# Recurrent states and outputs of a gated linear attention stage: another order on TensorE, state sums on another engine

## The chip, the cores and the metric

The kernel runs on one core of one Trainium2 chip. The metric is the device time of one execution in microseconds (us). TensorE (PE) multiplies matrices; its weight loads are shown as an engine of their own (PEld). VectorE (DVE), ScalarE (ACT) and GpSimd (POOL) work on whole tiles of 128 partitions; SyncE (SP) and ScalarE issue transfers. Matrix products land in PSUM. Everything here is float32.

## The reference

It is one step of a two-layer encoder over 656 tokens: a prompt of 528 (16 learned ones and 512 frames, from an empty state) and eight continued sequences of 16 tokens, each with a state of its own. Layer 0 mixes by gated linear attention (GLA), layer 1 by a gated short convolution; a causal convolutional feed-forward net of width 2816 follows each. The change touches only the GLA mixer, and of it what comes after the score matrices. For each of 4 heads (keys of 128, values of 256) the reference computes, for a block of tokens with start state S,

```python
def gla_chunk(S, q, k, v, g):
    b = jnp.cumsum(g, axis=1)
    o_inter = einsum('bthd,bhde->bthe', q * exp(b), S)
    ...
    A = einsum('bthd,bshd,btshd->bhts', q, k, decay)
    o_intra = einsum('bhts,bshe->bthe', A, v)
    b_last = b[:, -1]
    k_dec = k * exp(b_last[:, None] - b)
    S_new = exp(b_last)[..., None] * S + einsum('bshd,bshe->bhde', k_dec, v)
    return S_new, o_inter + o_intra
...
o = o * rsqrt(mean(o * o, axis=-1) + EPS) * head_gain      # the head norm
o = o.reshape(B, L, GLA_HV) * silu(r)
return o @ w_out, S
```

The states after the prompt (one a head) and after each sequence (eight a head) are outputs of the kernel too.

## The kernel before, in words

**Layout.** Activations lie as [128 channels, tokens]; 656 tokens are one tile row. A projection (`project`, L420) multiplies one unit of weights, 8 tiles of 128x128, with a high and a low part of both operands (three products each), 48 matmuls. Nearly the whole kernel is such units (196 of them), streamed in a ring of four.

**PSUM.** It is cut into four slots of two banks (1024 floats a partition). `plan_slots` hands them out in the order in which TensorE uses them, round robin: each step takes the next slot. Before a step TensorE waits in `open_slot` until the engine that read the slot's former content has raised `freed`. So the order of the steps also decides whose reader a step waits for: it is always the fourth step before it.

**The stage of states and outputs** comes after the last projection of values and gates (r, head 3, half 1) and its last score matrices A. The prompt is cut into four chunks of 128 tokens and a tail of 16. For each head h, TensorE does, in the order of `plan_slots`:

- U0: four updates, keys (tokens on partitions, tile `kd`) times values (`v_tok`), one of each chunk, [128 tokens] x [128 keys, 256 values] (L574)
- U1: four updates for sequences 0 to 3. The sample's 128 tokens are one tile; `kd` holds four copies of it, in each of which all but every fourth sequence is multiplied by zero (`C_FOURTH`), so that a matmul over 64 partitions gives the update of a single sequence
- the tail's update over 16 partitions, then U2 with sequences 4 to 7
- the head norm's sum of the head before (`head_norm(h-1)`, L582): ones times `osum`
- the transposes of the next head's keys (kT, L536)
- o0 and o1, the two halves of the outputs (L622): per chunk A times values and query times state (`chain`), and for each of the eight sequences a matmul of 16 columns with its old state (`s0`)

Slots, written as step: step whose reader frees it. In heads 1 and 2, head norm: U0, kT: U1, o0: tail, o1: U2, next U0: head norm.

**VectorE**, per head: `chain` (L975, L978: the running prompt state, one copy and three multiply-adds out of U0), four new states out of U1 (L991: old state times decay plus update), the tail's state (L998), four out of U2, then `finish(h-1)` (the inverse root of the head norm by one Newton step, L788 to L798, and two multiplications into `qk`, L967), then both halves of the outputs times gain and gate (`o32`, L1007) and the sum of squares `osum` (L1011).

**ScalarE**, per head: `head_root(h-1)` (logarithm and exponential, each time after a load of its table set), `k_to_tokens(h+1)` (kT out of PSUM into `kd`: one copy and four scaled copies, L1320, L1322), the stores of the states, the squares of both output halves (L1380), and `split_out(h-1)` (`oh`, L1241). At the head's end it issues the load of the states of head h+2. **GpSimd** subtracts `ol` = `qk` - `oh` (L378), which with `oh` is the input of w_out. The first projections of w_out (L646) take the k-th of 8 tiles when `o_done` says that `ol` is there.

**Ahead of the stage**, in head 3: ScalarE applies silu to the two gates with a table set of its own between the exponentials of the decays (`gate_r`), VectorE multiplies decays into k and q (`decayed`, steps 7 and 8) after the last gate, and the old states of heads 0 and 1 are loaded (L1358) into the space of the layer's input `xh` once the last projection is over.

Of the kernel before, what the change touches and what calls it, by code (L numbers as in the profile page):

```python
# [28 lines left out]
P = 128  # L29
# [21 lines left out]
RING = 4  # L51
# [25 lines left out]
C_FOURTH = 76  # L77
# [41 lines left out]
def plan_slots():  # L119
# [10 lines left out]
    for h in range(HEADS):  # L130
        s.straight(("U", h, 0), ("U", h, 1), ("U", h, "tail"), ("U", h, 2))
        if h:
            s.straight(("head_norm", h - 1))
        if h + 1 < HEADS:
            s.straight(("kT", h + 1))
        s.straight(("o", h, 0), ("o", h, 1))
# [27 lines left out]
def build(nc, x_in, w_in, wgd_in, wgu_in, par_in, reset_in, mask_in, s0_in, zc_in,  # L164
# [6 lines left out]
    def sb(name, shape, dt=F32, offset=None, size=None):  # L171
# [4 lines left out]
        for d in shape[1:]:  # L176
# [55 lines left out]
    kd = sb("kd", [P, 9, P], offset=b_at)  # L232
    chain = sb("chain", [P, 5, DV], offset=b_at + 9 * 4 * P)
    assert 9 * 4 * P + 5 * 4 * DV <= HEADS * T4
# [28 lines left out]
             "lev_done", "r_silu", "dec_done", "chain_stored", "osq_done", "osum_done", "o_done", "o_scaled", "oh_done", "x_back",  # L263
# [89 lines left out]
    def _(pool):  # L353
# [22 lines left out]
        for k in range(KT):  # L376
            pool.wait_ge(sem["oh_done"], k + 1)
            pool.tensor_tensor(ol[:, k, :], qk[:, k, :], oh[:, k, :].bitcast(F32),  # L378
                               ALU.subtract).then_inc(sem["o_done"], 1)
# [14 lines left out]
    def _(pe):  # L394
# [16 lines left out]
        def project(step, hi, lo, n_ready, ring, first=0, cut=HALF, i=0, release=1, before=None):  # L411
# [3 lines left out]
            for k in range(KT):  # L415
                if before:
                    before(k)
                for w, v in ((wh, hi), (wh, lo), (wl, hi)):
                    for c, a, z in banks(first, cut):
# [3 lines left out]
                        if k == 0 and w is wh and v is hi and c and release:  # L423
                            mm.then_inc(sem["units_used"], release)
            mm.then_inc(filled[p], 1)
# [113 lines left out]
        def value(kind, h, e):  # L539
            nonlocal n_unit  # L540
            project((kind, h, e), xh, xl, n_unit + 1, n_unit % RING)
            n_unit += 1
# [42 lines left out]
        for h in range(HEADS):  # L585
# [10 lines left out]
            for j in (1, 2):  # L596
                if j == 2:
                    open_slot(("U", h, "tail"))
                    mm, p = update(h, "tail", 0, kd[0:16, 4, :], v_tok[0:16, 4, vs])
                    mm.then_inc(filled[p], 1)  # L600
                open_slot(("U", h, j))
                for n in range(4):
                    s = 4 * (j - 1) + n
                    rows = slice(64 * (s // 4), 64 * (s // 4) + 64)
                    mm, p = update(h, j, n, kd[rows, 5 + s % 4, :], v_tok[rows, 5, vs])
                mm.then_inc(filled[p], 1)
            if h:
                head_norm(h - 1)
            if h + 1 < HEADS:
                transpose_k(h + 1)  # L610
            copied(("U", h, 0))
# [147 lines left out]
    def _(dve):  # L759
# [178 lines left out]
        for h in range(HEADS):  # L938
# [7 lines left out]
            for n, (kind, e) in enumerate((("v", 0), ("v", 1), ("r", 0), ("r", 1))):  # L946
                take_value(kind, h, e)
# [4 lines left out]
                decayed(h, 2 * n + 1)  # L952
# [6 lines left out]
                decayed(h, 2 * n + 2)  # L959
# [9 lines left out]

        dve.wait_ge(sem["dec_done"], HEADS)  # L970
        for h in range(HEADS):
            if h:
                dve.wait_ge(sem["chain_stored"], 16 * h)
# [10 lines left out]
            dve.wait_ge(s0_in_s[h % 2], 16 * (h // 2 + 1))  # L984
            if h >= 2:
                dve.wait_ge(snew_stored[h % 2], 16)
            for s in range(SEQS):
                n = s % 4
                if n == 0:
                    p = take(("U", h, 1 + s // 4))  # L990
                ins = dve.scalar_tensor_tensor(out=snew[:, h % 2, s, :], in0=s0[:, h % 2, s, :],  # L991
                                               scalar=dec[:, h, 5 + s:6 + s], in1=ps[:, p, n * DV:(n + 1) * DV],
                                               op0=ALU.mult, op1=ALU.add)
                if n == 3:
                    ins.then_inc(freed[p], 1)
                if s == 3:
                    p = take(("U", h, "tail"))
                    dve.scalar_tensor_tensor(out=chain[:, 4, :], in0=chain[:, 3, :], scalar=dec[:, h, 4:5],  # L998
                                             in1=ps[:, p, 0:DV], op0=ALU.mult, op1=ALU.add).then_inc(freed[p], 1)
            if h:  # L1000
                finish(h - 1)
            for e in range(2):
                p = take(("o", h, e))
                dve.wait_ge(sem["osq_done"], 2 * h + e + 1)
                if e == 0:
# [4 lines left out]
                                         op1=ALU.mult).then_inc(freed[p], 1)  # L1010
            dve.tensor_tensor(osum[:, :], osq[:, 0, :], osq[:, 1, :], ALU.add).then_inc(sem["osum_done"], 1)  # L1011
        finish(HEADS - 1)
        dve.wait_ge(sem["x_back"], 16)
# [188 lines left out]
    def _(act):  # L1202
# [23 lines left out]
        def root(step, r, d):  # L1226

            act.preload_act_table_set(LOG_EXP)
            inverse_root(two(r), slot(take(step)), r, d)
# [4 lines left out]
        def head_root(h):  # L1234
            root(("head_norm", h), head_std, DV)
# [82 lines left out]
        def k_to_tokens(h):  # L1318
            p = take(("kT", h))
            act.copy(kd[:, 0:5, :], blocks(ps[:, p, 0:5 * P], P))  # L1320
            for j in range(4):
                last = act.activation(kd[:, 5 + j, :], ps[:, p, 5 * P:6 * P], ACT.Copy,  # L1322
                                      scale=par[:, C_FOURTH + j:C_FOURTH + j + 1])
# [6 lines left out]
        for h in range(HEADS):  # L1330
# [13 lines left out]
            gate_r(h, 0)  # L1344
# [3 lines left out]
            gate_r(h, 1)  # L1348
            if h + 1 < HEADS:
                high(u + 3)  # L1350
# [8 lines left out]

        take(("r", HEADS - 1, 1))  # L1360
        load_states(0)
        load_states(1)
# [285 lines left out]
```

## Time and profile before

| | us |
|---|---|
| median of 3 timed runs | 1551.24 |
| lowest and highest | 1548.32, 1552.26 |
| the profiled execution's own time | 1546.99 |
| its span, first to last instruction | 1545.2 |
| TensorE busy in it | 1523.1 (99%) |
| VectorE, ScalarE, GpSimd busy | 1028.9, 441.1, 562.3 |

The profiled execution took 1.8 us more than its span. All times of rows are from the start of that span. A matmul of float32 operands is recorded as two instructions, each with a weight load: "x26" are 13 products. Ends of matmuls are modelled, and TensorE is shown busy where a matmul waits in the array, so the starts of the weight loads (PEld) tell the pace better. "[0.33 <-issue]" is idle time before an instruction for which no releaser was found. PEclk is the share of TensorE's full clock that was granted.

### The profile page before, as it was taken

The numbers are of one execution on the slowest core, as the hardware profiler recorded it, in microseconds if no ns is written. First come the engines' busy times: TensorE is split into PE (matmuls) and PEld (weight loads), VectorE is DVE, ScalarE is ACT, GpSimd is POOL, SyncE is SP. The second block draws the span as 40 slices with busy tenths as digits, with TensorE's granted clock in tenths as the row PEclk, the third lists the DMA queues.
The fourth block names the chain that finished last, engine by engine and source line by source line (L and its number), as shares of the span: only waits on it lengthen the run. The fifth ranks groups of instructions, "written<-read, shape, count | busy, mean of one in ns | idle before, by whom it ended". The sixth has DMA issues, their size and how long they took to land.

```text
span 1545.2 us, 26347 instructions
## 1 busy us (share of the span) xinstructions
PE 1523.1 (99%) x10294; PEld 1505.0 (97%) x10294; DVE 1028.9 (67%) x1495; ACT 441.1 (29%) x692; POOL 562.3 (36%) x397
## 2 busy tenths in 40 slices
PE   7999999999999999999999999999999999999997
PEld 6999998899999999999999999999999999999996
DVE  6566665744976676666669535548976676667667
ACT  5355554343222212212125111115221212212213
POOL 3532221143343434334342343432443344334340
PEclk9999999999999999999999999999999999999998
DMA  6211116222222222222221322222222222222212
GB/s 220 78 55 56 55 55 240 89 66 77 69 69 82 68 81 65 70 81 68 81 70 55 107 82 69 71 80 73 71 79 75 76 81 66 70 81 68 82 42 79
DMA packets 34841, 123.76 MB, mean 80 GB/s; under 512 B 3888, under 2 KB 6832, under 8 KB 33616
## 3 DMA queue, kind: packets, MB, share of 16 engines
q1 hardware_dynamic: 31840, 108.37, 22.0%
q10 hardware_dynamic: 2928, 14.35, 2.5%
q8 instruction: 54, 0.88, 0.2%
q14 instruction: 19, 0.16, 0.0%
HBM read 114.48 MB, written 8.22 MB: 79 GB/s over the span
## 4 chain that ended last, share of the span: by engine, by line
PE 96%; DVE 2%; ACT 1%; DVEq 1%; DMA 0%; POOL 0%; issue 0%; SPq 0%; ACTq 0%
PE ps L420 64%; PE ps L436 22%; PE ps L522 2%; PE ps L622 2%; PE ps L721 1%; PE ps L574 1%; PE ps L646 1%; PE ps L536 1%; DMA raw<-w_units 0%; DVE x L1177 0%; PE ps L656 0%; PE ps L503 0%; ACT xh L1214 0%; PE ps L493 0%; DVE sq L781 0%; DVEq L976 0%
## 5 line engine op out<-in xcount | busy, mean ns | idle before, releaser
L365 POOL TENSOR_TENSOR wl<-raw,wh 128x512 fp32r<-128x512 f32 x380 | 546.0, 1461 | 883.6 <-ACT wh L1260 846.9
L420 PE MATMUL ps<-xh,wh 128*128 128x320 f32 (+2 forms) x2144 | 494.5, 312 | 0.0
L420 PE MATMUL ps<-xl,wh 128*128 128x320 f32 (+2 forms) x2144 | 491.3, 310 | 0.0
L420 PE MATMUL ps<-xh,wl 128*128 128x320 f32 (+2 forms) x2144 | 490.8, 310 | 0.0
L420 PEld LDWEIGHTS ps<-xl,wh 128*128 128x128 f32 x2144 | 372.1, 188 | 0.0
L420 PEld LDWEIGHTS ps<-xh,wh 128*128 128x128 f32 x2144 | 369.9, 188 | 0.7
L420 PEld LDWEIGHTS ps<-xh,wl 128*128 128x128 f32 x2144 | 370.3, 188 | 0.0
L1260 ACT ACTIVATE wh<-raw 128x1024 fp32r<-128x1024 f32 x196 | 204.3, 1055 | 317.9 <-PE ps L420 294.4
L812 DVE TENSOR_TENSOR x<-ps,x 128x320 f32<-128x320 f32 (+2 forms) x320 | 167.5, 569 | 107.0 <-PE ps L436 78.1
L1025 DVE SCALAR_TENSOR_TENSOR y<-zp,par,y 128x660 f32<-128x660 f32 (+1 forms) x192 | 181.5, 945 | 28.0 <-issue 23.2
L436 PE MATMUL ps<-gh,wh 128*128 128x320 f32 (+1 forms) x768 | 175.6, 310 | 0.0
L436 PE MATMUL ps<-gh,wl 128*128 128x320 f32 (+1 forms) x768 | 175.1, 309 | 0.0
L436 PE MATMUL ps<-gl,wh 128*128 128x320 f32 (+1 forms) x768 | 174.8, 309 | 0.0
L1405 ACT COPY zl<-zp 128x18 f32 (+1 forms) x88 | 18.3, 208 | 533.5 <-DVE y L1025 533.5
L436 PEld LDWEIGHTS ps<-gh,wh 128*128 128x128 f32 x768 | 129.2, 188 | 0.0
L436 PEld LDWEIGHTS ps<-gl,wh 128*128 128x128 f32 x768 | 129.2, 188 | 0.0
L436 PEld LDWEIGHTS ps<-gh,wl 128*128 128x128 f32 x768 | 128.4, 188 | 0.0
L1021 DVE TENSOR_SCALAR y<-zp,par 128x660 f32<-128x660 f32 (+1 forms) x96 | 71.8, 748 | 29.8 <-issue 26.9
L1038 DVE TENSOR_TENSOR gl<-hh,gh 128x644 fp32r<-128x644 f32 (+1 forms) x52 | 84.0, 1615 | 3.9
L1044 DVE TENSOR_TENSOR zp<-ps,rstd 128x520 f32<-128x520 f32 x44 | 30.6, 696 | 58.6 <-PE ps L420 58.5
L1047 DVE TENSOR_TENSOR zp<-ps,rstd 128x320 f32<-128x320 f32 x44 | 21.5, 488 | 56.0 <-PE ps L420 55.8
L1036 DVE CAST gh<-hh 128x644 fp32r<-128x644 f32 (+1 forms) x52 | 48.2, 927 | 3.8
(160 smaller groups left out, 1283.6 us busy)
## 6 DMA issues: line engine op xcount, KB each, us to landing
raw<-w_units SPq DMA_DIRECT2D x196, 512.0 KB, 3.5
s<-states ACTq DMA_DIRECT2D x4, 1024.0 KB, 5.1
state_sample<-snew ACTq DMA_DIRECT2D x4, 1024.0 KB, 4.2
x<-x_t SPq DMA_DIRECT2D x8, 328.0 KB, 8.3
x<-x_t ACTq DMA_DIRECT2D x1, 2624.0 KB, 10.6
y_t<-x SPq DMA_DIRECT2D x4, 384.0 KB, 2.4
y_t<-x SPq DMA_DIRECT2D x4, 256.0 KB, 2.2
ffn_last<-zl ACTq DMA_DIRECT2D x2, 396.0 KB, 3.4
```

The source lines that it names most:

```text
L365: last = pool.tensor_tensor(wl[:, j, ks, :], raw[:, j, ks, :], wh[:, j, ks, :].bitcast(F32), ALU.subtract)
L420: mm = pe.matmul(ps[:, p, c:c + z - a], w[:, ring, k, :], v[:, k, a:z], start=(k == 0 and w is wh and v is hi), stop=(k == KT - 1 and w is ...
L436: mm = pe.matmul(ps[:, p, c:c + z - a], w[:, rings[f], m, :], v[:, f0 + f, a:z], start=(f == 0 and w is wh and v is gh), stop=(f == 1 and ...
L522: return pe.matmul(queries(ps[:, p, :], a, z), ks[:, a:a + P], queries(qs, a, z), start=True, stop=True)
L622: return pe.matmul(ps[:, p, a:z], lhsT, rhs, start=start, stop=stop, skip_group_check=True)
L812: last = dve.tensor_tensor(tile, product, tile, ALU.add)
L1021: dve.tensor_scalar(out, src[:, first:YN], w_col(0), w_col(3) if bias else None, ALU.mult, ALU.add if bias else ALU.bypass)
L1025: last = dve.scalar_tensor_tensor(out=out, in0=src[:, first + j:YN + j], scalar=w_col(j), in1=out, op0=ALU.mult, op1=ALU.add)
L1036: dve.tensor_copy(gh[:, f, first:TOK], hh[:, first:TOK])
L1038: dve.tensor_tensor(gl[:, f, first:TOK], hh[:, first:TOK], gh[:, f, first:TOK].bitcast(F32), ALU.subtract).then_inc(sem["g_done"], 1)
L1044: dve.tensor_tensor(two(zp[:, zi, 2 + first:SB]), slot(p, cut - first), two(factor[:, first:PROMPT]), ALU.mult)
L1260: act.activation(wh[:, j, :, :], raw[:, j, :, :], ACT.Copy).then_inc(sem["hi_done"], 1)
```

## The change

- **Order on TensorE and slots**: per head now U0, tail, head norm of the head before, key transposes, then U1 and U2, then o0 and o1. By the rule of the fourth step before, in heads 1 and 2 U1 now takes the slot of U0, U2 that of the tail, o0 that of the head norm, o1 that of kT; the next U0 takes that of U1, the next tail that of U2.
- **Sequence updates**: `kd` holds two masked copies in place of four (even and odd sequences, `C_PARITY`). Each update spans 32 partitions, two sequences of which one is zero. The eight go out in the order of partitions 0, 32, 64, 96 for the even sequences, then again for the odd ones; the four of a round write to four PSUM banks. Both slots are opened before the first of them.
- **New states**: ScalarE multiplies the old states by their decay into `snew` (`scale_states`, eight activations of 128x256 per head), and VectorE adds U1 and U2 in two additions of 128x1024. The tail's state is computed ahead of these, and has a buffer for even and for odd heads, so that `chain` waits only for the store of two heads ago.
- **ol**: the subtractions move from GpSimd to VectorE (`low_out`), between the two output halves of the next head; ScalarE's `split_out` moves to between its two squares.
- **Tables and loads**: only the first head norm loads its table set. In head 3 both silus come after the exponentials, `decayed` 7 and 8 before the last gate is taken, and the loads of the old states are issued when the last projection has used the first tiles of its input (semaphore `inputs_used`, raised after tiles 3 and 6).
- `k_to_tokens(h+1)` now also waits for U2 of head h, as `kd` is read longer.

```diff
     for h in range(HEADS):
-        s.straight(("U", h, 0), ("U", h, 1), ("U", h, "tail"), ("U", h, 2))
+        s.straight(("U", h, 0), ("U", h, "tail"))
...
             s.straight(("kT", h + 1))
-        s.straight(("o", h, 0), ("o", h, 1))
+        s.straight(("U", h, 1), ("U", h, 2), ("o", h, 0), ("o", h, 1))
...
     osum = sb("osum", [P, TOK], offset=xh_at + 32768 + 2 * T4)
-    kd = sb("kd", [P, 9, P], offset=b_at)
-    chain = sb("chain", [P, 5, DV], offset=b_at + 9 * 4 * P)
-    assert 9 * 4 * P + 5 * 4 * DV <= HEADS * T4
+    kd = sb("kd", [P, 7, P], offset=b_at)
+    chain = sb("chain", [P, 6, DV], offset=b_at + 7 * 4 * P)
+    assert 7 * 4 * P + 6 * 4 * DV <= HEADS * T4
...
                 low(j, RING * i + (RING + j + 1))
-        for k in range(KT):
-            pool.wait_ge(sem["oh_done"], k + 1)
-            pool.tensor_tensor(ol[:, k, :], qk[:, k, :], oh[:, k, :].bitcast(F32),
-                               ALU.subtract).then_inc(sem["o_done"], 1)
...
             assert done % RING == u % RING == 0
...
-        def project(step, hi, lo, n_ready, ring, first=0, cut=HALF, i=0, release=1, before=None):
+        def project(step, hi, lo, n_ready, ring, first=0, cut=HALF, i=0, release=1, before=None, marks=()):
...
             weights(n_ready)
...
                             mm.then_inc(sem["units_used"], release)
+                if k in marks:
+                    mm.then_inc(sem["inputs_used"], 1)
...
         def project_down(step, first, f0, n_ready, rings, i=0, release=1, g_count=None):
...
             nonlocal n_unit
-            project((kind, h, e), xh, xl, n_unit + 1, n_unit % RING)
+            project((kind, h, e), xh, xl, n_unit + 1, n_unit % RING,
+                    marks=(3, 6) if (kind, h, e) == ("r", HEADS - 1, 1) else ())
...
         def transpose_v(h, e):
...
             mm.then_inc(filled[p], 1)
-            for j in (1, 2):
-                if j == 2:
-                    open_slot(("U", h, "tail"))
-                    mm, p = update(h, "tail", 0, kd[0:16, 4, :], v_tok[0:16, 4, vs])
-                    mm.then_inc(filled[p], 1)
-                open_slot(("U", h, j))
-                for n in range(4):
-                    s = 4 * (j - 1) + n
-                    rows = slice(64 * (s // 4), 64 * (s // 4) + 64)
-                    mm, p = update(h, j, n, kd[rows, 5 + s % 4, :], v_tok[rows, 5, vs])
-                mm.then_inc(filled[p], 1)
+            open_slot(("U", h, "tail"))
+            mm, p = update(h, "tail", 0, kd[0:16, 4, :], v_tok[0:16, 4, vs])
+            mm.then_inc(filled[p], 1)
...
                 transpose_k(h + 1)
+            open_slot(("U", h, 1))
+            open_slot(("U", h, 2))
+            for odd in range(2):
+                for group in range(4):
+                    rows = slice(32 * group, 32 * group + 32)
+                    mm, p = update(h, 1 + group // 2, group % 2 * 2 + odd, kd[rows, 5 + odd, :], v_tok[rows, 5, vs])
+                    if odd and group % 2:
+                        mm.then_inc(filled[p], 1)
...
             pe.wait_ge(sem["lev_done"], 9 * h + 9)
...
             for n, (kind, e) in enumerate((("v", 0), ("v", 1), ("r", 0), ("r", 1))):
+                early = n == 3 and h == HEADS - 1
+                if early:
+                    dve.drain()
+                    decayed(h, 7)
+                    decayed(h, 8)
...
                     distance(h, 2 * n + 2)
-                decayed(h, 2 * n + 1)
+                if not early:
+                    decayed(h, 2 * n + 1)
...
                     distance(h, 2 * n + 3)
-                decayed(h, 2 * n + 2)
+                if not early:
+                    decayed(h, 2 * n + 2)
...
+        def low_out(h):
+
+            for k in (2 * h, 2 * h + 1):
+                dve.wait_ge(sem["oh_done"], k + 1)
+                dve.tensor_tensor(ol[:, k, :], qk[:, k, :], oh[:, k, :].bitcast(F32),
+                                  ALU.subtract).then_inc(sem["o_done"], 1)
...
         for h in range(HEADS):
-            if h:
-                dve.wait_ge(sem["chain_stored"], 16 * h)
+            if h > 1:
+                dve.wait_ge(sem["chain_stored"], 16 * (h - 1))
...
             dve.drain()
...
                 dve.drain()
-            dve.wait_ge(s0_in_s[h % 2], 16 * (h // 2 + 1))
-            if h >= 2:
-                dve.wait_ge(snew_stored[h % 2], 16)
-            for s in range(SEQS):
-                n = s % 4
-                if n == 0:
-                    p = take(("U", h, 1 + s // 4))
-                ins = dve.scalar_tensor_tensor(out=snew[:, h % 2, s, :], in0=s0[:, h % 2, s, :],
-                                               scalar=dec[:, h, 5 + s:6 + s], in1=ps[:, p, n * DV:(n + 1) * DV],
-                                               op0=ALU.mult, op1=ALU.add)
-                if n == 3:
-                    ins.then_inc(freed[p], 1)
-                if s == 3:
-                    p = take(("U", h, "tail"))
-                    dve.scalar_tensor_tensor(out=chain[:, 4, :], in0=chain[:, 3, :], scalar=dec[:, h, 4:5],
-                                             in1=ps[:, p, 0:DV], op0=ALU.mult, op1=ALU.add).then_inc(freed[p], 1)
+            p = take(("U", h, "tail"))
+            dve.scalar_tensor_tensor(out=chain[:, 4 + h % 2, :], in0=chain[:, 3, :], scalar=dec[:, h, 4:5],
+                                     in1=ps[:, p, 0:DV], op0=ALU.mult, op1=ALU.add).then_inc(freed[p], 1)
+            dve.wait_ge(sem["states_scaled"], h + 1)
+            for j in range(2):
+                p = take(("U", h, 1 + j))
+                states = snew[:, h % 2, 4 * j:4 * j + 4, :].rearrange("p s v -> p (s v)")
+                dve.tensor_tensor(states, ps[:, p, :], states, ALU.add).then_inc(freed[p], 1)
...
             for e in range(2):
...
                                          op1=ALU.mult).then_inc(freed[p], 1)
+                if h and e == 0:
+                    low_out(h - 1)
...
         finish(HEADS - 1)
+        low_out(HEADS - 1)
...
         update_x(lambda m: ("w_out", m), FIRST_ATT, 1)
...
-        def root(step, r, d):
-
-            act.preload_act_table_set(LOG_EXP)
+        def root(step, r, d, load=True):
+
+            if load:
+                act.preload_act_table_set(LOG_EXP)
...
         def head_root(h):
-            root(("head_norm", h), head_std, DV)
+            root(("head_norm", h), head_std, DV, load=h == 0)
...
             p = take(("kT", h))
+            if h:
+                take(("U", h - 1, 2))
             act.copy(kd[:, 0:5, :], blocks(ps[:, p, 0:5 * P], P))
-            for j in range(4):
+            for j in range(2):
                 last = act.activation(kd[:, 5 + j, :], ps[:, p, 5 * P:6 * P], ACT.Copy,
-                                      scale=par[:, C_FOURTH + j:C_FOURTH + j + 1])
+                                      scale=par[:, C_PARITY + j:C_PARITY + j + 1])
...
         def gate_r(h, e):
...
                 k_to_tokens(0)
-            gate_r(h, 0)
+            else:
+                gate_r(h, 0)
...
             decay(h, 7)
-            gate_r(h, 1)
             if h + 1 < HEADS:
+                gate_r(h, 1)
...
             act.activation(dec[:, h, 0:4], blocks(b[:, h, 0:TAIL], CH)[:, :, CH - 1], ACT.Exp, scale=1.0 / TAU)
...
+        def scale_states(h):
+
+            act.wait_ge(s0_in_s[h % 2], 16 * (h // 2 + 1))
+            if h >= 2:
+                act.wait_ge(snew_stored[h % 2], 16)
+            for n in range(SEQS):
+                last = act.activation(snew[:, h % 2, n, :], s0[:, h % 2, n, :], ACT.Copy,
+                                      scale=dec[:, h, 5 + n:6 + n])
+            last.then_inc(sem["states_scaled"], 1)
+
+        for h in range(2):
+            act.wait_ge(sem["inputs_used"], h + 1)
+            load_states(h)
+        gate_r(HEADS - 1, 0)
+        gate_r(HEADS - 1, 1)
+        act.drain()
         take(("r", HEADS - 1, 1))
-        load_states(0)
-        load_states(1)
+        scale_states(0)
...
         act.drain()
...
             copied(("U", h, 2))
-            act.dma_start(sp_out[:, h, :], chain[:, 4, :]).then_inc(sem["chain_stored"], 16)
+            act.dma_start(sp_out[:, h, :], chain[:, 4 + h % 2, :]).then_inc(sem["chain_stored"], 16)
             act.dma_start(ss_out[:, h, :, :], snew[:, h % 2, :, :]).then_inc(snew_stored[h % 2], 16)
+            if 0 < h < HEADS - 1:
+                scale_states(h + 1)
...
                 act.activation(osq[:, e, :], ps[:, p, 0:TOK], ACT.Square).then_inc(sem["osq_done"], 1)
-            if h:
-                split_out(h - 1)
+                if e == 0 and h:
+                    split_out(h - 1)
+                if e == 0 and h == 0:
+                    scale_states(1)
...
         act.dma_start(zc[:, :, :], zc_in).then_inc(sem["zc_in"], 16)
...
     par[:, C_CCACHE:N_PAR] = a["cache_conv"][0].reshape(SEQS, 2, KT, P).transpose(3, 2, 0, 1).reshape(P, -1)
-    for j in range(4):
-        par[:, C_FOURTH + j] = np.arange(P) // SLEN % 4 == j
+    for j in range(2):
+        par[:, C_PARITY + j] = np.arange(P) // SLEN % 2 == j
...
     wgu = np.concatenate([a["gla_w_gate_up"][0]] * 2)
```

## Rows read from the trace of the kernel before

**Rows 1.** The page: header, and shares by engine of the last chain.

```profile
span 1545.2 us, 26347 instructions
PE 96%; DVE 2%; ACT 1%; DVEq 1%; DMA 0%; POOL 0%; issue 0%; SPq 0%; ACTq 0%
```

**Rows 2.** Windows by head: start:end, length, busy each engine, PEclk, DMA share, GB/s.

```profile
239.30:255.30 16.00, 15.88 (x107) 13.55 (x106) 8.32 (x17) 5.92 (x12) 2.51 (x2) 1.00 0.97 369
255.30:275.20 19.90, 19.90 (x109) 16.57 (x109) 13.14 (x22) 5.90 (x10) 0.00 (x0) 0.83 0.38 142
275.20:292.30 17.10, 16.95 (x110) 14.16 (x109) 14.11 (x22) 7.18 (x12) 3.71 (x2) 1.00 0.35 131
292.30:308.80 16.50, 16.36 (x104) 13.57 (x103) 14.11 (x22) 5.55 (x7) 3.70 (x2) 1.00 0.18 72
```

**Rows 3.** Timeline, head 2, TensorE: start, us, engine, line, operation, operands, count.

```profile
275.23 6.44 PE L574 MATMUL ps<-v_tok,kd 128*128 128x256 f32 x26
...
277.13 1.59 PEld L574 LDWEIGHTS ps<-v_tok,kd 64*128 64x128 f32 x8 [0.33 <-issue]
...
279.68 1.59 PEld L574 LDWEIGHTS ps<-v_tok,kd 64*128 64x128 f32 x8 [0.33 <-issue]
...
281.60 1.37 PE L582 MATMUL ps<-osum,ones 128*128 128x328 f32 x4
...
283.12 0.85 PE L536 MATMUL ps<-ident,qk 128*128 128x128 f32 x6
...
283.80 0.61 PE L622 MATMUL ps<-AT,v_tok 128*128 128x128 f32 x4
```

**Rows 4.** Timeline, head 2, the other engines.

```profile
275.42 0.72 ACT L1380 ACTIVATE osq<-ps 128x656 f32<-128x656 f32 x1 [5.15 <-PE ps L622]
...
276.24 0.90 DVE L1007 SCALAR_TENSOR_TENSOR o<-ps,par,sr 128x656 f32<-128x656 f32 x1 [4.31 <-ACT osq L1380]
...
276.85 3.71 POOL L378 TENSOR_TENSOR ol<-qk,oh 128x656 fp32r<-128x656 f32 x2 [30.29 <-ACT oh L1241]
277.05 2.07 DVE L1011 TENSOR_TENSOR osum<-osq 128x656 f32<-128x656 f32 x1
...
279.05 0.41 DVE L975 COPY chain<-ps 128x256 f32<-128x256 f32 x1
...
279.53 1.59 DVE L978 SCALAR_TENSOR_TENSOR chain<-chain,dec,ps 128x256 f32<-128x256 f32 x3
...
281.32 1.66 DVE L991 SCALAR_TENSOR_TENSOR snew<-s,dec,ps 128x256 f32<-128x256 f32 x4 [0.19 <-issue]
...
282.89 0.47 DVE L998 SCALAR_TENSOR_TENSOR chain<-chain,dec,ps 128x256 f32<-128x256 f32 x1
...
284.85 0.90 DVE L788 TENSOR_SCALAR osum<-ps,par 128x656 f32<-128x656 f32 x1
```

**Rows 5.** Timeline, head 1: the same sum of squares with GpSimd idle.

```profile
257.08 0.83 DVE L1011 TENSOR_TENSOR osum<-osq 128x656 f32<-128x656 f32 x1
```

**Rows 6.** Groups by form, all four heads: count, busy us, mean ns, idle before.

```profile
L574 PE MATMUL ps<-v_tok,kd 64*128 64x256 f32 x64 | 16.4, 397 | 0.0
```

**Rows 7.** Timeline, head 0: sixteen weight loads for products of 16 columns.

```profile
249.13 1.87 PEld L622 LDWEIGHTS ps<-qk,s 128*128 128x128 f32 x16
```

**Rows 8.** Timeline, head 0: end of U0; ScalarE's scaled copies.

```profile
241.18 1.59 PEld L574 LDWEIGHTS ps<-v_tok,kd 64*128 64x128 f32 x8 [0.33 <-issue]
...
247.15 1.15 ACT L1322 ACTIVATE kd<-ps,par 128x128 f32<-128x128 f32 x4
```

**Rows 9.** DMA issues around the stage: KB each, median us to landing.

```profile
s<-states ACTq DMA_DIRECT2D x4, 1024.0 KB, 5.1
```

**Rows 10.** Window of 4 us in which the granted clock fell.

```profile
254.00:258.00 4.00, 4.00 (x21) 3.26 (x20) 1.65 (x2) 2.00 (x2) 0.00 (x0) 0.74 1.04 376
```

**Rows 11.** Timeline, w_out after head 3: GpSimd's ol and TensorE's wait for it.

```profile
310.46 3.75 POOL L378 TENSOR_TENSOR ol<-qk,oh 128x656 fp32r<-128x656 f32 x2 [12.80 <-ACT oh L1241]
...
314.27 0.30 PEld L646 LDWEIGHTS ps<-oh,wh 128*128 128x128 f32 x2 [1.00 <-POOL ol L378]
```

More of the change, by code:

```diff
@@ L76 @@
 C_SCW = 52
-C_FOURTH = 76
+C_PARITY = 76
 C_EPS, C_HALF_EPS = 80, 81
@@ L262, in build @@
              "xs_hi", "xs_lo", "sq_done", "sum_done", "log_done", "root_done", "soft_done", "mask_in", "d_done", "e_done",
-             "lev_done", "r_silu", "dec_done", "chain_stored", "osq_done", "osum_done", "o_done", "o_scaled", "oh_done", "x_back",
+             "lev_done", "r_silu", "dec_done", "inputs_used", "states_scaled", "chain_stored", "osq_done", "osum_done", "o_done", "o_scaled", "oh_done", "x_back",
              "zc_in", "pads_in", "y_done", "zl_saved", "gate_silu", "g_done", "cpads_in", "cy_done",
```

## The prediction, made before the changed kernel was run

> **What bounds the kernel now.** I read the page first. TensorE carries 96% of the chain that ended last in a span of 1545.2 us [rows 1], so only what shortens or lengthens TensorE's own sequence counts. The change touches the stretch from the first state update to the first w_out units. The windows by head divide it: 16.0, 19.9, 17.1 and 16.5 us for heads 0 to 3 [rows 2]. They show TensorE busy all through, but its records hide waits inside the array, so I read the timeline of one undisturbed head, head 2, by the starts of the weight loads. With T = 275.23, where its updates start: U0 is over at T+1.9, U1, tail and U2 at T+6.4, the head norm's sum runs 1.4 us, kT starts at T+7.9, the outputs at T+8.5 [rows 3], and the next head at T+17.1, so the outputs take 8.6. TensorE's own work thus sets the pace; kT alone waited a moment, for VectorE's states. VectorE in the same head: square of o1 until 276.14, o32 until 277.14, osum until 279.12, chain from 279.05 to 281.12, four states from 281.32 to 282.98, tail at 282.89, half_square (L788) at 284.85 [rows 4].
>
> **Step 1: the slots, and what TensorE waits for now.** All of head h in heads 1 and 2, T as above.
> VectorE: o32 ends at T+1.9 as before. osum took 2.07 beside GpSimd's ol [rows 4] and 0.83 with GpSimd idle [rows 5]; ol leaves GpSimd, so I take 0.83: osum ends at T+2.65. The chain's 2.07 us run from T+2.6 to T+4.7, then 0.2 for the drain (281.12 to 281.32) and 0.47 for the tail: T+5.35.
> TensorE: U0 1.9, tail 0.63 (U2's load at 279.68, less U1's at 277.13 and U1's 1.92), so T+2.55. The head norm waits for osum until T+2.8 and takes 1.37, kT 0.66: T+4.8. U1 and U2 now need the slots of U0 and the tail, both opened first: they wait until T+5.35+0.14 = T+5.5 (0.14 lies between the states' end at 282.98 and kT at 283.12).
> The eight updates: see step 2, 1.9 or 3.4 us; the last ends at T+7.4 or T+8.9.
> Then the new wait: o0 takes the slot of the head norm, which VectorE frees with half_square, and half_square stands behind both additions. An addition of 128x1024 is not in the trace; from 0.47 us at 256 columns and 0.90 at 656 [rows 4] it is 0.47 + 768 x 0.00107 = 1.3 us, two back to back 2.45. Bounds: 1.9, if they cost no more per column than the 0.83 of osum at 656, with start-up shared, and 2.6. The first starts when U1 is filled, at six of the eight updates: T+7.0 or T+8.1. Additions to T+9.4 or T+10.5, half_square to T+10.2 or T+11.4, outputs from T+10.3 or T+11.5, next head at T+18.9 or T+20.1. Before it was 17.1. So heads 1 and 2 lose 1.8 each, 3.6 together, or 3.0 each, 6.0 together. Queued behind the waiting o0 is all of TensorE; the stall of some 2.7 us stands in nobody's cover. The head norm's logarithm on ScalarE can start at T+4.2, needs about the 0.72 of a square, and is not late.
>
> **Step 2: do updates of different partitions overlap?** The trace has none in such an order. Lower end of their speed: instructions over 64 partitions have 397 ns each [rows 6], and U1's eight take 1.9 us as U0's over 128 do [rows 3]: a product on fewer rows is no cheaper, 0.213 us per instruction, eight products 3.4 us. Upper end: where products are short (16 columns), sixteen weight loads follow in 1.87 us [rows 7], 0.11 each; the sixteen loads of eight updates can't come faster, 1.8 us. Each float32 product is two instructions on the same rows, which must follow each other, while the next product's first has other rows and another bank free: a pipeline two wide, 8 x 0.213 + 0.2 = 1.9 us. I take 1.9, at the end of the row of weight loads, since the order leaves nothing shared between neighbours but that load path; 3.4 is the rival's.
> The Trainium skill (TensorE: Matmul & The Clock Gate, Part 3) says that products at different row groups run concurrently, 3.07 times as fast for four of 32 rows and 512 columns; by that figure, estimated, the eight would take 1.1 us instead of 3.4 and the sum below would be 3 us lower. No row of this case shows it. On the other side TensorEngine Tiling (Key Properties) says that changing the tiling mode drains the array; the trace agrees: each change between 128 and fewer partitions shows 0.33 us before the load [rows 3], and there are four a head before and after, which changes nothing.
>
> **Step 3: heads 0 and 3.** Head 0: U0 is over at 241.2 [rows 8]; q and k are ready earlier than before, so the chain runs 241.2 to 243.3, the updates from 243.4 to 245.3 (or 246.8), the outputs 8.7: 254.0 (or 255.5) against 255.3. Gain 1.3 (or loss 0.2). The additions need scale_states: eight activations of 256 columns, 0.39 each (0.29 at 128, 1.15 for four [rows 8], 0.72 at 656), 3.1 us on ScalarE after the states land. Their load is issued before 239 and takes 5.1 [rows 9], so they are scaled at 245 to 247, and kT's copy after them is done before o1 wants its slot at 249.7. If they land later, o1 waits 1 or 2 us. In later heads this lies beside the outputs and costs nothing. Head 3 has no kT: o0 has the tail's slot, o1 the head norm's, so it waits for the chain alone: updates from T+4.8 to T+6.7 (8.3), outputs to T+15.5 (17.0) against 16.5. Gain 1.0 (loss 0.5).
>
> **Step 4: the clock.** From 254 to 258, after output products of 16 columns, the mean grant was 0.74 [rows 10]; over head 1 it was 0.83, which is 6.8 us at the level of 1.2 GHz, and head 1 took 19.9 where head 2 at 2.4 GHz took 17.1 [rows 2]: 2.8 us. Afterwards heads 1 and 2 have some 0.7 and 2.8 us without work ahead of their outputs, so I expect half as much again, 10 us at the lower level, +1.4. Bounds: none of it, -2.8, and two and a half times as much, +4.2.
>
> **Step 5: the end.** TensorE waited 1.0 us for ol behind 3.75 us of GpSimd [rows 11]. On VectorE ol of head 2 is done before the last head's outputs end: -1.0. ol of head 3 takes VectorE 0.83 each (as osum) in place of GpSimd's 1.9, so it is earlier, beside the same early products of w_out that hid it before. ScalarE's dropped table loads and copies and the earlier loads lie beside TensorE and are worth nothing but step 3's.
>
> **Sum**, overlapping: +3.6 - 1.3 - 1.0 + 1.4 - 1.0 = +1.7 us. The profiled execution's own time, 1546.99, lies 4.3 under the median of the runs, which is above all of the difference; I add to the median: 1551.24 + 1.7 = 1553.
>
> **The rivals.**
> A, the forecast, updates overlap two wide: +1.7, 1553 (its own range 1549 to 1556), chance 0.46.
> B, the slower side: the updates do not overlap. +6.0 + 0.5 + 0.2 + 0.7 (the idle time before the outputs is a little shorter) - 1.0 = +6.4, 1557.6. It decides from the point where the eight updates take over 3 us. For it: 397 ns at 64 partitions. Against: those never alternated. 0.27.
> C, faster: four updates overlap fully (1.0 us, -0.9 in each of 4 heads) and the clock never falls (-4.2 against step 4): 1.7 - 3.6 - 4.2 = -6.1, 1545. For it: heads 2 and 3 ran whole at full clock. Against: idle time is added, and a float32 product's two halves use the same rows. 0.17. The rule of the Trainium skill in step 2 (TensorE: Matmul & The Clock Gate, Part 3) is on its side.
> D: the updates overlap as in A, but the stalls bring the lower clock in every head, and the state load is late: +4.2 - 1.4 + 1.5 on A's 1.7, +6.0, 1557. 0.10.
>
> **The numbers.** About 0.3% (4.7 us) is what a measurement of this kernel can tell from no change. Faster: C and a little of A, 0.20. Slower: B and D less what falls inside, and A's edge, 0.33. Same 0.47. Range 1545 to 1560: it holds A, B, D and the near half of C.
>
> **What would show it.** Right, if in heads 1 and 2 o0's first weight load follows the last update by over 2 us and starts with the end of L788; if the sixteen update instructions of U1 and U2 start within 2 us; if osum takes 0.83 everywhere; and if no wait stands in the first w_out unit. Heads 1 and 2 near 19 us, 0 near 15, 3 near 15.5. Wrong, if the outputs start before half_square ends, or if additions of 1024 columns take well under 1.2 us.

## The result, and the profile after

The changed kernel is slower: 1557.64 us median (1555.28 to 1563.45, 19 runs) against 1548.32 us (1542.67 to 1553.60, 19 runs), ratio 1.0068 with a 95% interval of 1.0055 to 1.0081, some 10.5 us; the two medians lie 9.3 us apart. The forecast was 1553 in a range of 1545 to 1560, "the same" at 0.47 and slower at 0.33. Ratios are to the kernel before, timed beside each kernel, and the difference between two changed kernels is that of their ratios. Two disturbed executions, one of the kernel before at 6330.47 us and one of a variant at 1574.75, are left out of the ratios. The page of the profiled execution, its header and the shares of the last chain:

```profile
span 1557.5 us, 26352 instructions
PE 96%; DVE 2%; ACT 1%; DVEq 1%; DMA 0%; issue 0%; SPq 0%; ACTq 0%
```

The span grew by 12.3 us, and TensorE is still the chain [rows 1]. The windows of heads 0 to 3 and of the first three w_out units say where (columns as in [rows 2]):

```profile
238.70:254.30 15.60, 14.66 (x106) 12.91 (x106) 6.05 (x9) 9.96 (x22) 2.49 (x2) 0.89 0.80 289
254.30:278.40 24.10, 19.91 (x111) 17.56 (x111) 13.59 (x18) 10.07 (x18) 0.00 (x0) 0.72 0.37 150
278.40:306.90 28.50, 25.08 (x109) 21.28 (x109) 13.68 (x18) 8.82 (x18) 0.00 (x0) 0.57 0.21 79
306.90:322.40 15.50, 15.09 (x103) 12.47 (x104) 12.17 (x17) 4.46 (x6) 0.00 (x0) 0.90 0.19 77
322.40:345.00 22.60, 22.60 (x150) 22.25 (x150) 12.17 (x16) 6.22 (x9) 0.00 (x0) 1.00 0.09 33
```

Heads 1 and 2 took 52.6 us in place of 37.0 [rows 2]; heads 0 and 3 gained 1.4 together, the first units of w_out 1.2 (22.6 against 23.8), and the stage starts 0.6 earlier. The granted clock is the column that changed most: 0.72 and 0.57. A grant of 0.50 is 1.2 GHz and one of 1.00 is 2.4 GHz, so in each window (1 - grant) x length x 2 is the time at the lower level: 3.4, 13.5, 24.5 and 3.1, together 44 us where it was 6.8.

The timeline of head 1 (T = 254.27), TensorE and VectorE, to be read against [rows 3, 4]:

```profile
254.27 1.60 PEld L573 LDWEIGHTS ps<-v_tok,kd 128*128 128x128 f32 x8
...
256.12 0.83 DVE L1018 TENSOR_TENSOR osum<-osq 128x656 f32<-128x656 f32 x1
...
257.07 0.85 PEld L581 LDWEIGHTS ps<-osum,ones 128*128 128x128 f32 x4 [0.58 <-issue]
...
259.05 0.48 DVE L998 SCALAR_TENSOR_TENSOR chain<-chain,dec,ps 128x256 f32<-128x256 f32 x1
...
259.65 0.77 PEld L573 LDWEIGHTS ps<-v_tok,kd 32*128 32x128 f32 x16 [0.79 <-DVE chain L991]
259.68 1.15 PE L573 MATMUL ps<-v_tok,kd 32*128 32x256 f32 x16 [0.58 <-DVE chain L998]
...
260.92 2.36 DVE L1004 TENSOR_TENSOR snew<-ps,snew 128x1024 f32<-128x1024 f32 x2 [1.39 <-PE ps L573]
...
263.19 0.89 DVE L787 TENSOR_SCALAR osum<-ps,par 128x656 f32<-128x656 f32 x1
...
264.23 1.20 PE L621 MATMUL ps<-AT,v_tok 128*128 128x128 f32 x4 [3.40 <-DVE osum L787]
```

The reader is to see two things. The last row names its releaser: the outputs waited 3.40 us for half_square (L787), which stood behind the two additions (L1004). And the eight updates, sixteen instructions, took 1.15 us. What came after the wait stands in the chain that ended last (start, us, what), both output halves of heads 1, 2 and 3:

```profile
264.23 14.15 PE ps L621 x72
...
290.50 16.33 PE ps L621 x72
...
313.72 8.72 PE ps L621 x72
```

The same 72 instructions take 8.7 us at full clock, and 1.6 and 1.9 times as long behind the two waits.

Finer windows show where the clock fell and came back (start:end and length as above, the granted clock third from the end):

```profile
246.70:250.70 4.00, 4.00 (x29) 4.00 (x28) 0.90 (x1) 2.25 (x6) 1.60 (x2) 0.72 1.04 415
...
270.70:274.70 4.00, 4.00 (x20) 4.00 (x20) 1.31 (x2) 1.99 (x3) 0.00 (x0) 0.50 0.00 0
274.70:278.70 4.00, 4.00 (x29) 3.72 (x29) 1.09 (x2) 0.28 (x1) 0.00 (x0) 0.87 0.00 0
278.70:282.70 4.00, 4.00 (x10) 2.39 (x10) 3.02 (x5) 0.43 (x1) 0.00 (x0) 0.56 0.73 262
...
302.70:306.70 4.00, 4.00 (x21) 4.00 (x20) 0.00 (x0) 0.00 (x0) 0.00 (x0) 0.50 0.00 0
```

There are four spells at the lower level. Two of them began inside the two waits and lasted some 13.6 and 20.5 us, 34 of the 44; in the second of these TensorE was busy without a break from 290.5 to 309.9 and the clock stayed down. The other two began while TensorE was busy: 3.4 us in the outputs of head 0, and 6.8 us from U0 of head 2, after the clock had come back before the outputs of head 1 were over. Spells of that shorter kind stand in the kernel before as well, as [rows 10] shows one.

### The profile page after: what moved, and what is told of

It is laid out like the page before. It is cut to its first block, busy times and chain, and to the rows that moved or that the text cites. A ratio compares the mean times of both kernels' runs of the same rounds, so it can differ in the third digit from the quotient of the medians.

```text
span 1557.5 us, 26352 instructions
## 1 busy us (share of the span) xinstructions
PE 1528.1 (98%) x10294; PEld 1511.4 (97%) x10294; DVE 1028.4 (66%) x1479; ACT 444.7 (29%) x710; POOL 547.9 (35%) x389
## 4 chain that ended last, share of the span: by engine, by line
PE 96%; DVE 2%; ACT 1%; DVEq 1%; DMA 0%; issue 0%; SPq 0%; ACTq 0%
PE ps L416 63%; PE ps L434 22%; PE ps L621 3%; PE ps L520 2%; PE ps L720 1%; PE ps L645 1%; PE ps L573 1%; PE ps L534 0%; DMA raw<-w_units 0%; DVE x L1185 0%; PE ps L655 0%; PE ps L501 0%; ACT xh L1222 0%; PE ps L491 0%; DVEq L792 0%; DVE sq L780 0%
```

## The experiments

Of each kernel "lower-clock time" is worked out from its windows as above. Theory W and rival C are those of the expectations below; this rival C is not the prediction's.

**half_square ahead of the additions.** Base: the changed kernel.

```diff
             p = take(("U", h, "tail"))
 ...
+            if h:
+                q = take(("head_norm", h - 1))
+                half_square(..., two(osum[:, :]), slot(q), DV).then_inc(freed[q], 1)
             dve.wait_ge(sem["states_scaled"], h + 1)
             for j in range(2):
...
-            inverse_root(("head_norm", h), head_std, osum[:, :], DV)
+            refine(ROOT_ORDER.index(("head_norm", h)), head_std, osum[:, :])    # heads 0 to 2
```

> Only VectorE's order changes: half_square of the head norm before goes ahead of the two additions of 128x1024, so the slot that o0 wants in heads 1 and 2 is freed by about T+6.3 instead of T+9.9. Theory W (the wait for half_square starts the loss, the lower clock follows from the idle time): o0 starts some 0.2 us after the last update, 3.4 us of wait go in each of two heads, most of the lower clock with them (under 12 us at the lower level in the stage, against 44 in the changed kernel); heads 1 and 2 near 15.5 us each; time 14 to 18 us below the changed kernel, 5 to 9 below the one before. Rival C (the clock falls because the updates are now only 1.15 us of dense work and the outputs with 16 columns are not enough, whatever waits there are): the wait goes, -7 us, but the outputs stay at the lower clock, heads 1 and 2 at 19 to 22 us; time 7 us below the changed kernel, 2 to 3 above the one before.

Measured: 1540.80 us against 1547.02 for the kernel before, ratio 0.9953 (0.9935 to 0.9970), 6 runs. That is 1.15% or 18 us below the changed kernel and 7 us below the one before; it beats both. Windows of its heads 0 to 3:

```profile
238.90:253.00 14.10, 13.16 (x106) 11.51 (x106) 6.05 (x9) 9.91 (x22) 2.49 (x2) 1.00 0.81 292
253.00:268.10 15.10, 14.32 (x110) 12.23 (x110) 12.44 (x17) 9.96 (x18) 0.00 (x0) 1.00 0.66 265
268.10:285.60 17.50, 17.50 (x110) 14.05 (x110) 13.69 (x19) 8.69 (x17) 0.00 (x0) 0.80 0.34 129
285.60:301.10 15.50, 15.23 (x103) 12.48 (x104) 13.82 (x19) 4.50 (x6) 0.00 (x0) 0.89 0.19 77
```

and in its head 1 the outputs now follow the updates at once, with the additions beside them:

```profile
258.24 1.15 PE L573 MATMUL ps<-v_tok,kd 32*128 32x256 f32 x16 [0.58 <-DVE chain L1001]
259.31 0.52 PEld L621 LDWEIGHTS ps<-AT,v_tok 128*128 128x128 f32 x4 [0.33 <-issue]
...
259.48 2.36 DVE L1010 TENSOR_TENSOR snew<-ps,snew 128x1024 f32<-128x1024 f32 x2 [0.57 <-PE ps L573]
```

Lower-clock time is 10 us, as expected under 12. Theory W holds, rival C (outputs stay slow) falls: the outputs of heads 1 to 3 took 8.7 us each. But head 2 took 17.5 us and not 15.5, since the spells that are left begin at the end of a head's outputs, about the U0 of heads 2 and 3, with TensorE busy.

**Keep TensorE busy in the wait.** Base: the changed kernel. It computes seven products that nobody reads.

```diff
+            if h in (1, 2):
+                pk, _ = slots.at(("kT", h + 1))
+                for _ in range(7):
+                    mm = pe.matmul(ps[:, pk, 768:1024], ones[:, :], v_tok[:, 0, vs], start=True, stop=True, ...)
+                mm.then_inc(filled[pk], 1)        # kT of heads 2 and 3 is passed on only here
```

> The changed kernel with seven products of 256 columns (3.0 us at full clock) that nobody reads put into heads 1 and 2 where TensorE waits for half_square, into columns of the key transposes' slot that are not used; that slot is passed to ScalarE after them. The wait itself stays as long as it was. Theory W: the idle time is what lowers the clock, so with it filled the heads 1 and 2 take about 18.6 us each in place of 24.1 and 28.5, and the time falls by 10 to 15 us although nothing waits less. Rival C: the clock falls as before (outputs 14 to 16 us), the time is the same or up to 3 us more.

Measured: 1546.90 us against 1547.02, ratio 0.9999 (0.9984 to 1.0014), 12 runs; 0.69% or 10.7 us below the changed kernel, although the outputs start no earlier behind the updates. Head 1, TensorE, and the windows of heads 1 and 2:

```profile
259.06 1.15 PE L574 MATMUL ps<-v_tok,kd 32*128 32x256 f32 x16 [0.58 <-DVE chain L1005]
...
260.14 3.29 PE L614 MATMUL ps<-v_tok,ones 128*128 128x256 f32 x14
...
263.61 0.68 PE L628 MATMUL ps<-AT,v_tok 128*128 128x128 f32 x4 [0.18 <-DVE osum L794]
```

```profile
253.80:272.40 18.60, 17.63 (x124) 14.87 (x124) 13.59 (x18) 9.95 (x18) 0.00 (x0) 1.00 0.53 216
272.40:292.10 19.70, 19.20 (x123) 15.71 (x123) 13.68 (x18) 8.68 (x18) 0.00 (x0) 0.91 0.31 114
```

The outputs are still held up by half_square (L794), but run at full clock: heads 1 and 2 take 18.6 and 19.7 us in place of 24.1 and 28.5, at grants of 1.00 and 0.91 in place of 0.72 and 0.57. This splits the price of the slot order, 17.8 us between the changed kernel and half_square ahead: 10.7 us is the clock that the two idle waits took away, and the other 7.1 (half_square ahead against this kernel, 0.9953 and 0.9999) is about the two waits of 3.4 us themselves. The split is no finer than some 3 us either way, by the intervals of the ratios.

**The order of the eight updates.** Base: the changed kernel.

```diff
-            for odd in range(2):
-                for group in range(4):
+            for group in range(4):
+                for odd in range(2):
```

> The eight updates of a head in another order: both of the same 32 rows and the same bank one after the other, in place of four different ones in turn. If neighbours on other rows overlap and those on the same rows do not, the eight take 2.0 to 3.4 us in place of 1.15 and each head is later by 1 to 2 us from this, +4 to +8 us at an equal clock. If the 1.15 us came from something else (32 rows being cheaper), they stay at 1.15. The clock may move it either way by some us, since TensorE is busy longer and idle no longer: theory W has no opinion beyond 5 us.

Measured: 1558.78 us against 1547.02, ratio 1.0070 (1.0049 to 1.0092), 4 runs: the time of the changed kernel. The updates take the same time, in the chain of head 0:

```profile
243.06 1.17 PE ps L573 x16
```

My expectation that neighbours on the same rows cost 2 us or more fell. Either 32 rows are cheap, or the groups run side by side whatever the order; the next one tells.

**All eight on the same rows.** Base: half_square ahead. Six of the eight new states of each head are left out: the rows of the first two stand in for theirs.

```diff
-                    rows = slice(32 * group, 32 * group + 32)
+                    rows = slice(0, 32)
```

> The kernel with half_square first, but all eight updates of each head taken from partitions 0 to 31 (the new states of six of eight sequences are thus not those of the reference). The order of the updates made no difference to their 1.15 us. If groups of rows work side by side, each group paced by its own two products, eight products on one group take 8 x 0.43 = 3.4 us. If a product over 32 rows is simply cheaper than one over 64 or 128, they take 1.15 us again.

Measured, a single run: 1565.30 us. The chain in heads 1 to 3:

```profile
268.59 3.69 PE ps L573 x16
...
289.28 3.69 PE ps L573 x16
...
312.16 3.69 PE ps L573 x16
```

So a product over 32 rows is not cheaper; four groups of rows run side by side, and 1.15 us fits each being paced by its own two products (2 x 0.43 = 0.85, plus the start). That the order does not matter fits TensorE issuing on to a group that is free; no row shows this by itself. The time, some 24 us above its base, holds 2.5 us for the updates in each of heads 1 to 3 and, again, the clock: it fell in all four heads.

**The cheaper updates alone.** Base: the kernel before.

```diff
-                for n in range(4):
-                    s = 4 * (j - 1) + n
-                    rows = slice(64 * (s // 4), 64 * (s // 4) + 64)
-                    mm, p = update(h, j, n, kd[rows, 5 + s % 4, :], v_tok[rows, 5, vs])
+                for odd in range(2):
+                    for g in range(2):
+                        group = 2 * (j - 1) + g
+                        rows = slice(32 * group, 32 * group + 32)
+                        mm, p = update(h, j, 2 * g + odd, kd[rows, 5 + odd, :], v_tok[rows, 5, vs])
```

> The kernel before with one part of the change alone: two masked copies of the keys in place of four, and updates over 32 partitions, in the old order of steps and slots. U1 and U2 go from 1.9 us to about 1.1 each. Theory: it gives almost nothing in heads 1 and 2, since kT wants U1's slot, which VectorE frees with the fourth new state at T+6.6 to T+7.9 whatever TensorE does: heads 1 and 2 gain under 0.7 us each, heads 0 and 3 about 0 to 1.5, 0 to 3 us in all at an equal clock, and the new idle time can lower the clock and take it back. Rival (the gain of the fast version comes from the cheaper updates alone): 6 to 7 us below the kernel before.

Measured: 1553.73 us against 1548.32, ratio 1.0028 (1.0014 to 1.0043), 12 runs: a loss of 4 us. Its timeline, head 2 and then head 1:

```profile
279.33 0.50 PEld L582 LDWEIGHTS ps<-osum,ones 128*128 128x128 f32 x2 [2.77 <-DVE chain L979]
```

```profile
264.15 0.85 PE L536 MATMUL ps<-ident,qk 128*128 128x128 f32 x6 [0.50 <-DVE snew L992]
```

TensorE is done sooner and then waits for VectorE's slots (the head norm for U0's, by the chain; kT for U1's, by the new states). In its chain the outputs of head 0 took 11.2 us and those of head 2 13.1 in place of 8.8 and 8.5, so the clock fell more. That the new idle time is the reason is the likely reading after the kernel with the wait filled, but it was not tested here. The rival, that the cheaper updates alone are the gain, falls.

**ol back on GpSimd.** Base: half_square ahead. The loop of L378 returns to GpSimd, `low_out` goes.

> The kernel with half_square first, and ol back on GpSimd. Theory: osum beside GpSimd's subtractions takes 2.07 us again in place of 0.83 in heads 2 and 3, each 1.2 us on the path now that the chain of prompt states ends last before the updates, and the wait of 0.7 to 1.0 us in the first w_out unit is back: +3 to +4 us over the kernel with half_square first, more if the clock falls once more. Rival: GpSimd hides it, under 1 us.

Measured: 1538.93 us against 1548.32, ratio 0.9936 (0.9917 to 0.9956), 6 runs; not above half_square ahead (0.9953). I expected +3 to +4 and was wrong. The timeline of its profiled execution (at 1544.63 us the slowest of the six), heads 2 and 3, tells why:

```profile
287.98 3.10 POOL L378 TENSOR_TENSOR ol<-qk,oh 128x656 fp32r<-128x656 f32 x2 [16.62 <-ACT oh L1257]
...
290.35 1.43 DVE L1026 TENSOR_TENSOR osum<-osq 128x656 f32<-128x656 f32 x1
```

```profile
303.87 3.14 POOL L378 TENSOR_TENSOR ol<-qk,oh 128x656 fp32r<-128x656 f32 x2 [12.79 <-ACT oh L1257]
307.13 0.83 DVE L1026 TENSOR_TENSOR osum<-osq 128x656 f32<-128x656 f32 x1
```

With `split_out` between ScalarE's two squares, GpSimd starts earlier and is out of osum's way, once wholly, once but for its end, and in its waits there is none of the first w_out unit for ol. So the engine is not what helps. The earlier `split_out` is left as the likely cause; no run moved it alone.

**Each slot waited for by itself.** Base: half_square ahead.

```diff
-            open_slot(("U", h, 1))
-            open_slot(("U", h, 2))
-            for odd in range(2):
-                for group in range(4):
+            for group in range(4):
+                if group % 2 == 0:
+                    open_slot(("U", h, 1 + group // 2))
+                for odd in range(2):
```

> The kernel with half_square first, with the updates of U1 (groups of rows 0 and 1) started once U1's slot is free, and those of U2 once the tail's is, in place of both waits ahead of all eight. The slots come free 0.55 us apart, so up to 0.5 us goes per head in heads 1 to 3: 1 to 2 us less than with half_square first, if the two halves still overlap; nothing or a loss of 1 us if the second half's wait costs a new start of 0.3 us each.

Measured: 1541.49 us against 1548.32, ratio 0.9945 (0.9924 to 0.9966), 6 runs: no difference to half_square ahead that these runs can show. The chain of its heads 2 and 3 has 1.71 us for the sixteen instructions in place of 1.15: two halves of two groups each take longer than four groups together, and this can take back what the earlier start wins.

**One product more before the updates.** Base: half_square ahead. One product of 256 columns behind each kT.

> The kernel with half_square first, and one product of 256 columns (0.43 us) that nobody reads behind each set of key transposes (heads 0 to 2), where TensorE stands before the updates for 0.6 to 0.8 us. It lies in that wait, so it costs nothing. Theory W (idle time decides the clock): fewer or shorter spells at the lower clock than with half_square first (three in its timed executions, judging by a mean grant of 0.991 to 0.994 over the whole), 1 to 3 us less. Rival C (the output products with 16 columns decide it): no difference beyond 1 us.

Measured: 1541.04 us against 1548.32, ratio 0.9940 (0.9919 to 0.9960), 6 runs. A gain of 1 to 3 us would be hidden in the noise, so the time alone does not decide; the grants do: its executions have means of 0.991 to 0.995, half_square ahead 0.991 to 0.994, and in its profile the outputs of head 2 took 11.64 us. So there are no fewer spells, and filling the waits of 0.6 to 0.8 us by some 0.4 does not take them away; this speaks against theory W in that small range. What does bring them stays open; they begin, as in the kernel before and in half_square ahead, while TensorE is busy.

**New states on VectorE again.** Base: half_square ahead, with the eight multiply-adds of L991 and without `scale_states`; `chain` waits again for the store of the head before.

> The kernel with half_square first, and the new states computed as in the kernel before: eight multiply-adds of 256 columns on VectorE straight from the loaded states and PSUM, no scaling on ScalarE. VectorE works 3.3 us on them in place of 2.4, behind half_square. Theory: with the slot of the head norm freed ahead, they are off the path and this part of the change was worth nothing: within 1.5 us of the kernel with half_square first. Rival (the split with ScalarE is what makes room on VectorE): VectorE is late for the next head's sum by about 1 us a head, +3 us or more.

Measured: 1538.69 us against 1548.32, ratio 0.9936 (0.9916 to 0.9957), 6 runs, the same as half_square ahead. The chain has its outputs of heads 1 to 3 at full clock:

```profile
259.16 8.72 PE ps L621 x72
...
276.64 8.73 PE ps L621 x72
...
292.23 8.72 PE ps L621 x72
```

Moving the scaling to ScalarE was worth nothing that these runs can show, as expected; behind half_square the states have room on either engine.

Half_square ahead and its four variants lie at 0.9936 to 0.9953, all below both kernels, and these runs do not tell them apart; by the intervals, two of them would have to lie some 4 us apart for that.

## Why the prediction was right and where it was wrong

**Step 1, the slots: right.** The wait was named with its place and releaser, and the outputs' first load was put at T+10.3; it came at T+9.9 (264.20). osum took 0.83 as forecast, the tail's state ended at T+5.3 (forecast 5.35), two additions took 2.36 us (forecast 2.45). The wait itself was longer than the forecast 2.7 us, 3.4, because the updates ahead of it were over sooner.

**Step 2, the updates: right in kind, mis-sized.** I took a pipeline two wide, 1.9 us; it is four wide, 1.15. The Trainium skill's rule (TensorE: Matmul & The Clock Gate, Part 3, products at different row groups run concurrently) holds here, for float32 too: 3.69 us on one group against 1.15 on four is 3.2 times, beside its 3.07. My reason against it, that a float32 product's two halves share their rows, bounds one group and not the four. Rival B (no overlap) is out.

**Step 3: right in kind.** Head 3 took 15.5 us as forecast. Head 0 took 15.6 and not near 15, since its outputs ran 3.4 us at the lower clock; at full clock, in half_square ahead, it took 14.1.

**Step 4, the clock: the step that failed.** The sum had +1.4 us for 10 us at the lower level, with bounds of -2.8 and +4.2; it was 44 us, and filling the waits gave back 10.7, outside these bounds. At full clock the changed kernel's heads 1 and 2 would take what they take with the wait filled, 18.6 and 19.7 us, close to the 18.9 of the sum; they took 24.1 and 28.5. I took the spells of the kernel before, 6.8 us, and added half as much again for the idle time. What the runs showed instead is that a wait of 3.4 us, the clock falling inside it, was followed by 10 to 20 us at 1.2 GHz although TensorE was busy again: through most of the outputs behind the first wait, and through the outputs and into the U0 of head 3 behind the second. Why the clock stayed down so long is open; that the 16-column products matter in it was not tested. Rival D named the mechanism (the stalls bring the lower clock, 1557) and had 0.10, but its late load of the states, 1.5 us, did not come, and its clock term of +4.2 was too small as well. B's time, 1557.6, came with B's reason refuted: its agreement with 1557.64 is chance.

**Step 5: right in size, partly for a wrong reason.** The first three w_out units took 22.6 us against 23.8, of which some 0.2 is a longer cut; the wait of [rows 11] is gone. The engine of ol is not the cause, as its return to GpSimd showed; the earlier `split_out` is the likely one.

**The sum.** Without its clock term the forecast was +0.3 us; the kernel with the waits filled, with the mean grant of the kernel before from 238 to 330 us (0.96), measured 0.9999, or -0.2. In that near zero a longer stall and shorter updates offset each other. The clock's 10.7 us on top is the measured loss.

**What was luck.** The forecast of +1.7 us came out at +10.5, and by the prediction's own limit of 0.3% this is "slower", which had 0.33, and not "the same", which had 0.47. The time lies inside the range of 1545 to 1560 partly because the forecast was laid on a median of three runs, 1551.24: nineteen runs gave 1548.32. On 1551.24 the measured ratio would have given 1561.8, outside it.

## What to carry to other kernels

A round-robin of PSUM slots makes each step wait for the reader of the step four before it; when steps are reordered, read that list anew and put the reader that frees the next slot first on its engine. One reordered instruction turned +0.68% into -0.47%. And an idle gap on TensorE is to be priced with the clock that it may cost the work behind it: here two gaps of 3.4 us cost about one and a half times their own length on top.

## What the runs showed of the hardware

- Float32 products over 32 partitions in four groups of rows took 1.15 us for eight of 256 columns (1.17 in the other order), 3.69 on a single group: the overlap is between groups, and it did not matter whether neighbours were of one group or of different ones.
- After an idle wait of 3.4 us the granted clock stayed at 1.2 GHz for 19 us of unbroken work (290.5 to 309.9 in the changed kernel), and with the same waits filled by seven unread products the time fell by 10.7 us.
- At the lower clock the sixteen weight loads before 16-column products took nearly twice their 1.87 us of [rows 7], as this row of the changed kernel's head 1 shows:

```profile
268.83 3.53 PEld L621 LDWEIGHTS ps<-qk,s 128*128 128x128 f32 x16
```
